# The sum over experts taken head by head: eight PSUM accumulations and eight VectorE additions per tile instead of one accumulation

## The reference, cut to what matters

```python
def block(args):
    xb, eb, gb = args            # 128 tokens, their experts (128, 8, 16), their gates
    ub = u_tab[eb]
    vb = v_tab[eb]
    act = jax.nn.gelu(jnp.einsum('td,thkd->thk', xb, ub), approximate=False)
    return jnp.einsum('thk,thkd->td', gb * act, vb)
...
h_lat = h_lat + g2 * y_lat
```

## Time and profile before

| | |
|---|---|
| runs of the kernel | 4520.79, 4525.88 and 4529.47 us, median 4525.88 |
| the profiled execution | 4520.79 us, its span in the profile 4519.0 us |
| TensorE, share of the span busy | 79% |
| VectorE | 61% |
| ScalarE | 26% |
| GpSimd | 34% |
| mean rate of the DMA | 322 GB/s over the span |
| mean granted TensorE clock | 0.931 of full speed |

### The profile page before, as it was taken

How to read it: one execution, slowest core, us unless ns; L and a number is a source line. 1 busy time by engine, 2 the same in 40 slices (tenths; PEclk the granted TensorE clock), 3 DMA queues, 4 the chain that set the end, 5 groups by cost and what they waited for, 6 DMA issues and landing times. The chain is left out here.

```text
span 4519.0 us, 38887 instructions
## 1 busy us (share of the span) xinstructions
PE 3574.6 (79%) x10024; PEld 1731.3 (38%) x10024; DVE 2775.2 (61%) x6957; ACT 1156.5 (26%) x2826; POOL 1527.8 (34%) x1338
## 2 busy tenths in 40 slices
PE   8899978778768768777777768996877876877776
PEld 1288643323323323323322227784332332332322
DVE  2222348776776676676676545664877677667654
ACT  1121013222222222222232122551322222222212
POOL 0102114444443444443344321000444444444432
PEclk9898589999999999998999998998999999999999
DMA  8712049999999999999999982003999999999998
GB/s 300 253 56 84 1 171 376 407 397 393 403 387 390 402 382 386 406 378 373 411 387 409 421 369 82 1 1 151 378 399 397 394 406 398 368 408 392 400 421 344
DMA packets 233035, 1455.51 MB, mean 322 GB/s; under 512 B 25140, under 2 KB 25140, under 8 KB 67812
## 3 DMA queue, kind: packets, MB, share of 16 engines
q0 software_dynamic: 184320, 1342.26, 73.2%
q1 hardware_dynamic: 48392, 110.79, 6.9%
q10 hardware_dynamic: 96, 0.10, 0.0%
HBM read 1447.72 MB, written 5.34 MB: 322 GB/s over the span
## 5 line engine op out<-in xcount | busy, mean ns | idle before, releaser
L1371 PE MATMUL peer_py<-peer_ring,peer_diag 128*128 128x512 f32 x5120 | 2470.4, 631 | 821.3 <-ACT peer_diag L1288 820.7
L1217 POOL DMA_INDIRECT peer_ring<-in_uv_dram,peer_idx x1280 | 1443.1, 1127 | 2008.6 <-PE peer_py L1371 1728.1
L1482 DVE CUSTOM_DVE_ANT_0 peer_ring<-peer_ring,peer_f 128x1024 f32<-128x1024 f32 x1280 | 1565.9, 1226 | 768.9 <-DMA peer_ring<-in_uv_dram,peer_idx 738.0
L1371 PEld LDWEIGHTS peer_py<-peer_ring,peer_diag 128*128 128x128 f32 x5120 | 983.0, 200 | 2277.4 <-ACT peer_diag L1288 1161.8
L1288 ACT ACTIVATE peer_diag<-ident,peer_coef 128x128 f32<-128x128 f32 x1280 | 443.9, 394 | 1813.0 <-DVE peer_coef L1458 1813.0
L1285 ACT ACTIVATE peer_gel<-peer_u 128x2 f32<-128x2 f32 x640 | 129.9, 203 | 711.4 <-DVE peer_u L1482 710.4
L318 DVE TENSOR_TENSOR m_w_low<-m_w_low_plain,m_w_high 128x2048 fp32r<-128x2048 f32 x26 | 61.0, 2347 | 218.5 <-ACT m_w_high L313 218.5
L1208 POOL IOTA peer_iota<- 128x16 f32 x2 | 0.3, 144 | 504.7 <-POOLq L765 363.9
L326 PE MATMUL m_ps<-m_w_high,m_aT_high 128*128 128x512 f32 x416 | 165.3, 397 | 3.3 <-DVE m_v L750 1.6
L326 PE MATMUL m_ps<-m_w_low,m_aT_high 128*128 128x512 f32 x416 | 163.1, 392 | 0.0
L326 PE MATMUL m_ps<-m_w_high,m_aT_low 128*128 128x512 f32 x368 | 144.5, 393 | 0.0
(11 more groups left out here) (196 smaller groups left out, 2824.9 us busy)
## 6 DMA issues: line engine op xcount, KB each, us to landing
arena<-in_ada_w_dram SPq DMA_DIRECT2D x16, 2048.0 KB, 8.8
peer_ring<-in_uv_dram,peer_idx POOLq DMA_INDIRECT x1280, 9.0
mod_rows_sb<-in_ada_w_dram SPq DMA_DIRECT2D x8, 2048.0 KB, 9.2
m_w_low_plain<-in_ev_w_in_dram SPq DMA_DIRECT2D x12, 1024.0 KB, 5.2
arena<-in_peer_wq_dram SPq DMA_DIRECT2D x2, 4096.0 KB, 19.2
mod_rows_sb<-mod_rows SPq DMA_DIRECT2D x7, 1024.0 KB, 7.1
m_w_low_plain<-in_od_w_in_dram SPq DMA_DIRECT2D x6, 1024.0 KB, 5.4
m_w_low_plain<-in_ev_w_out_dram SPq DMA_DIRECT2D x4, 1024.0 KB, 5.0
```

The lines of the kernel that those rows point to most:

```text
L1217: pool.indirect_dma_start(ring[:, s % RING], None, A["uv"], bass.IndirectOffsetOnAxis(idx[:, hd, j:j + 1], 0)).then_inc(sem(f"landed{s % R ...
L1371: ins = pe.matmul(PY[:, b], diag[:, s % RING], ring[:, s % RING, D + b * HALF:D + (b + 1) * HALF], start=s == 0, stop=s == TS - 1)
L1482: dve.tensor_tensor_reduce(x, x, f[:], 1.0, 0.0, ALU.mult, ALU.add, u[:, g % 4, j:j + 1]).then_inc(sem("dot"), 1)
```

## The change

`PY` becomes two pairs of banks. The slots of a head accumulate in one pair, the next head's in the other. When a head is complete, VectorE moves its sum out of PSUM: head 0 by a copy into `y`, heads 1 to 7 by an addition to `y` (`head_sum`). For heads 0 to 6 this stands behind the dots of pairs 11, 19, 27, 35, 43, 51 and 59, ahead of the routing piece of that pair; for head 7 at the end of the tile. TensorE waits for `y_free` at the start of each head, for the sum of the head two before it. The product with the gate row now reads `y` in SBUF and not PSUM, and raises a new semaphore, `gated`.

```diff
-        PY = ctx.enter_context(nc.psum_tensor(T + "py", [P, 2, HALF], F32))
+        PY = ctx.enter_context(nc.psum_tensor(T + "py", [P, 2, 2, HALF], F32))
...
             def body(i, now, nxt):
                 for g in range(PAIRS_T):
-                    if g == 0:
-                        pe.wait_ge(sem("y_free"), i + 1)
+                    hd = g // PAIRS
+                    if g % PAIRS == 0:
+                        pe.wait_ge(sem("y_free"), i * NH + hd + 1)
                     for j in range(PAIR):
                         s = PAIR * g + j
                         pe.wait_ge(sem("diag"), i * TS + s + 1)
                         for b in range(2):
-                            ins = pe.matmul(PY[:, b], diag[:, s % RING], ring[:, s % RING, D + b * HALF:D + (b + 1) * HALF],
-                                            start=s == 0, stop=s == TS - 1)
+                            ins = pe.matmul(PY[:, hd % 2, b], diag[:, s % RING], ring[:, s % RING, D + b * HALF:D + (b + 1) * HALF],
+                                            start=s % TOPK == 0, stop=s % TOPK == TOPK - 1)
...
+            def head_sum(i, hd):
+
+                dve.wait_ge(sem("slot_free"), i * TS + RING + (hd + 1) * TOPK)
+                ps = PY[:, hd % 2].rearrange("p b n -> p (b n)")
+                if hd == 0:
+                    dve.tensor_copy(y[:], ps).then_inc(sem("y_free"), 1)
+                else:
+                    dve.tensor_tensor(y[:], y[:], ps, ALU.add).then_inc(sem("y_free"), 1)
+
             if layer == 0:
-                dve.sem_inc(sem("y_free"), 1)
+                dve.sem_inc(sem("y_free"), 2)
...
+                    if g % PAIRS == 3 and g >= PAIRS:
+                        dve.wait_ge(sem("y_free"), i * NH + g // PAIRS + 1)
+                        head_sum(i, g // PAIRS - 1)
...
                 coefficients(i, PAIRS_T - 1)
-                dve.wait_ge(sem("slot_free"), i * TS + RING + TS)
+                dve.wait_ge(sem("y_free"), i * NH + NH + 1)
+                head_sum(i, NH - 1)
+                dve.wait_ge(sem("y_free"), i * NH + NH + 2)
+
                 if i is first:
                     dve.wait_ge(sem("gates"), 16 * rows_loads)
-                dve.tensor_tensor(y[:], PY[:].rearrange("p b n -> p (b n)"), rows[:, row_kind(i), 2], ALU.mult).then_inc(sem("y_free"), 1)
-                dve.wait_ge(sem("y_free"), i + 2)
+                dve.tensor_tensor(y[:], y[:], rows[:, row_kind(i), 2], ALU.mult).then_inc(sem("gated"), 1)
+                dve.wait_ge(sem("gated"), i + 1)
                 dve.tensor_tensor(h[:, i - shift], h[:, i - shift], y[:], ALU.add).then_inc(sem("h"), 1)
```

## The result

The changed kernel takes 4597.18 us (median of four runs, 4594.8 to 4603.24), the kernel before 4525.25 (four runs, 4520.79 to 4529.47). The ratio is 1.0166, 95% interval 1.0151 to 1.0180, or +72 us. The forecast was +46, with a range to 4597: the direction was right, and 26 us of the size are missing. The first question is where they lie.

What follows compares the result with a forecast made beforehand. The prediction took VectorE's program order as the bound in pairs 36 to 56, the gathers without routing, and a chain at tile ends. Terms 13.3 + 25.6 + 4.8 + 2.4 = 46.1 us on 4526 gave 4572, range 4552 to 4597.

Steps and rivals of the forecast that it cites:

- (a): Ten tile ends: head 7's sum lengthens the chain from last matmul to next dots; 13.3 us, between 12.2 and 13.7.
- (b): Pairs 35, 43, 51 in eight routing tiles: 24 sums of 1.2 us less 3.2 for the queue; 25.6 us, 18.4 to 32.9.
- The 2.18 us: Each sum's hold on VectorE by the skill's flush rule, in place of 1.2 us; the whole would then be 91 us.
- (c): Pairs 11 and 19 of tiles 0 and 6: four sums of 1.2 us with routing; 4.8 us, 2.3 to 5.5.
- (e): The other 34 sums, hidden in VectorE's waits for the DMA: nothing, at pair 59 up to 2 us in all.
- (d): Pair 11 in the other eight tiles: the gather delay just fits, 0.3 us each; 2.4 us, 0 to 9.6.
- The idle time at the loop's jump I leave as it is: At the loop's jump: the 5.58 us of idle before the copy of `f` stays unchanged, nothing added.
- nothing measurable: Rival: tile ends too are covered, by gathers still in flight; 4526 us, chance 0.04.
- faster: Rival: TensorE starts new tiles before `PY` is read, 1.22 us earlier at eight ends; 4516 us, chance 0.02.
- only the tile ends: Rival: delays inside a tile vanish in the gather queue, only ends cost 13 us; 4539 us, chance 0.08.
- every sum costs: Rival: gather-bound stretches have no real slack, so all 80 sums cost 1.2 us; 97 us, 4623, chance 0.03.
- holds VectorE for twice its length: Rival: each sum holds VectorE 2.45 us in place of 1.2; 103 us together, 4629, chance 0.02.

Runs made afterwards that it cites:

- e1: The kernel before with an added copy of PY to y at each tile's end, the product then reading y: 4544.27 us, ratio 1.0025 to the kernel before.
- e3: The changed kernel without the sums at pairs 35, 43 and 51: 4563.97 us, ratio 1.0072 to the kernel before.
- e7: The changed kernel with twelve semaphore increments, which do nothing and run once, ahead of the loop: 4591.64 us, ratio 1.0139 to the kernel before.
- e13: The kernel before with one unused 128x1024 VectorE addition from SBUF at pair 27 of each tile: 4527.53 us, ratio 1.0003.
- e4: The changed kernel without the sums at pairs 19, 27 and 59: 4587.84 us, ratio 1.0130 to the kernel before.
- e8: The kernel before with one unused 128x1024 VectorE addition from SBUF at pair 11 of each tile: 4541.25 us, ratio 1.0034.
- e5: The changed kernel with each sum inside a tile three pairs later (14, 22, ..., 62): 4581.59 us, ratio 1.0127 to the kernel before.
- e2: The changed kernel without the sums at pair 11: 4587.37 us, ratio 1.0119 to the kernel before.
- e11: The changed kernel with four unused TensorE matmuls at pair 10 in the eight tiles that route for a successor: 4599.36 us, ratio 1.0159 to the kernel before.
- e12: The changed kernel with the edits of e5 and e7 together: 4578.43 us, ratio 1.0109 to the kernel before.

## Why the prediction was right or wrong

**Right: (a).** Tile ends. 11 to 14 us alone (e1) against 13.3; per end 1.25 us written out, 1.46 in the loop (forecast 1.265 and 1.375).

**Right: (b).** Pairs 35, 43 and 51. 24.0 to 25.9 us in four traces, 30 by the times of e3 and e7 (33 with e3's rest of the stop), against 25.6. VectorE's order was the bound there. The deduction of 3.2 for the queue was a guess, and no run tests it alone; that the sum comes so close is in part luck. The 2.18 us would have made it 49: the flush rule of the Trainium skill, VectorE: DVE Perf Modes, section "The DRAIN you can't avoid", does not hold for a sum. The section itself excepts an operation that is not held, and the trace agrees with the exception: the instruction behind a sum starts 1.13 us after it.

**Right: (c) and (e).** 5.1 to 6.3 us against 4.8. The 34 sums taken as free are free as far as can be told: pairs 26 to 33 and the tiles 5 and 9 lie at or below zero, e13 gives 1 us (-3 to 6); e4's 4 to 6 us, of which 2.4 are pair 19 in tiles 0 and 6, have too wide an interval to say more. One trace has 8.7 us in pairs 57 to 63, another 2.5, a third 0.4; what happened in the first isn't known.

**Wrong in size: (d), "a delay of 1.2 just fits. I take 0.3 each".** It measured 17 to 20 us for eight tiles, where I had 2.4 and an upper end of 9.6. The slack that I worked out was not one. I took the 6.93 us from the issue of slot 30's gather to its dot, less 5.45 for a gather issued to idle queues, as time in which it could come later. In e8 the gather is issued 0.59 us before the dot of slot 28 instead of 1.95, 1.36 later, and the dot of slot 30 comes 1.44 later: from issue to dot it is 7.01 us, no less than before. All of a delay comes through. In the changed kernel's tile 2, where the issue is later still, the DMA engines go dry behind it (0.51 busy over 4 us); in e8's they are busy 0.96 and pass 348 GB/s in place of 418, and why the delay comes through there too is not shown. The upper end was too low as well, since a late gather comes with more than one delay.

I sorted tiles by when slot 30's gather was issued: the eight tiles of row (d), in eight traces without an instruction added at pair 11 and six with one. In the table are the pairs 14 to 26 in us, means over the tiles; gathers at full rate would need 12 x 4.97 = 59.6:

```
slot 30's gather issued, after
pair 12's first dot                4.65 to 4.72 us    5.07 to 6.51 us
nothing added at pair 11           60.37 (45 tiles)   61.81 (19 tiles)
one instruction added              61.54 (20 tiles)   63.54 (28 tiles)
```

Down a column it is 1.2 and 1.7 us, the delay itself. Along a row it is 1.4 and 2.0 us, and with the addition 28 of 48 tiles fall into the dearer class instead of 19 of 64. The delay, 1.2 to 1.7, and 0.29 x 1.8 = 0.5 make about 1.9 us a tile, 15 us for eight. By the times it is 13 to 18 us: e8's 15 less 2.4 for tiles 0 and 6, e5's 18, and e2's 18 with its stop taken off, less the same 2.4. That the delay is what costs is shown, by e8 (put in) and by e5 and e2 (taken away).

That the dearer class comes of the clock is shown by the same 14 traces, by the clock over the matmuls themselves. In all 112 tiles pair 11's matmuls begin 1.85 to 1.92 us after the first dot of pair 12, and the gather is issued 0.97 to 1.02 us after the four of slot 22, which free its buffer. In the 65 tiles of the first column these four take 1.82 us at a granted clock of 1.00, in the 47 of the second 2.20 to 3.58 us at 0.50 to 0.83; no tile falls between. (The lower level alone does not tell: 47 of the 65 had it too for a while, but earlier, as in tile 2 of the kernel before at pair 10.) And e11's six tiles with the clock at 1.00 show, in one trace, that an issue made late by other means is as dear. Two things stay open. Why the lower level meets pair 11 more often with the addition, 28 times in 48 against 19 in 64, is not shown: the idle time ahead of pair 11's matmuls was 1.93 to 4.64 us in the late tiles and 0.76 to 3.77 in the others. And only two tiles, in e11, had the clock kept up there without a delay from the filler.

**Left out: "The idle time at the loop's jump I leave as it is".** This is the second step that failed. The 5.6 us there are indeed unchanged (22.4 us at four jumps, 22.5 before), but behind them came another stop of 4.0 to 4.6 us at three jumps, 13 us in all, a wait that the sum put at nothing. e7 shows what decides it: not what the sums do but where in the code the loop begins. In e2, with one sum less ahead of the loop, it stands one instruction later and is 3 us long; in e3 and e4, with three less, 0.8 to 1.0 us are left of it behind the third dot. That the engine waits there for its instructions to be fetched is the reading that fits, but no run shows it; which boundary the loop's start crossed isn't known, and so I could not have said whether this change would meet it.

**The whole.** By the times: ends 12, the stop 12, pairs with routing 33 (25 by the traces), pair 11 in all tiles 15, pair 19 in tiles 0 and 6 another 2, together 74, or 66 by the traces' 25. Measured were 72 and 77, each with an interval of some 7 us on either side. The kernel is slower for the reason that was given, and the increase is over half as much again for two terms that stood at 2.4 and at nothing. Of the rivals, "nothing measurable" and "faster" fall by the result, "only the tile ends" by rows (b) and (d), "every sum costs" by e13 and "holds VectorE for twice its length" by the starts 1.13 us apart.

None of the versions beats the kernel before. The best of those that have all sums is e12, 1.1% slower: three sums a tile stand where VectorE is the bound, and one at the end of the chain.

## What to carry to other kernels

Time from issue to use, less the shortest such time seen, is not slack: here a gather issued 1.36 us later was used 1.44 us later. Where an instruction is added ahead of a transfer that an engine is soon going to wait for, price the delay in full, and look whether it comes with a second one, as here by TensorE's clock (1.82 or up to 3.58 us for the same four matmuls). In a chain that runs from a dot through a matmul to the next gather, the place of an instruction decides: the same 1.2 us cost 1.6 us at pair 11 and next to nothing at pairs 14 or 27. When code is added to a kernel with hardware loops, look at the first instructions behind each jump before explaining the rest, several of them, since a stop can move behind the next one, and compare ablations only between kernels with the same stops there.

## What was not expected of the hardware

A jump of a hardware loop costs VectorE 5.4 to 6.2 us of idle time in each of the kernels here, and a further 3.6 to 4.6 us ahead of the next instruction in some: 4.59, 4.33 and 4.00 in one trace, 4.59, 4.31 and 4.35 in another, 2.9 to 3.2 us one instruction later still in e2, and none at all with twelve small instructions more ahead of the loop (1.0168 against 1.0139).

Addition and product of 128x1024 float32 take the same with an operand in PSUM (1.216 and 1.225 us) as from SBUF alone (1.220 in e8, 1.225 in the changed kernel). A copy does not: 1.221 us out of PSUM, 0.69 us from SBUF to SBUF, as that of `f`.

TensorE's matmuls behind a wait of 4.64 us began at 0.50 of the full clock where those behind one of 0.94 us ran at 1.00: sixteen matmuls took 9.75 us there and 7.13 here.

```profile
1444.43 9.75 PE L1372 MATMUL peer_py<-peer_ring,peer_diag 128*128 128x512 f32 x16 [4.64 <-ACT peer_diag L1288]
```

```profile
1415.34 7.13 PE L1371 MATMUL peer_py<-peer_ring,peer_diag 128*128 128x512 f32 x16 [0.94 <-ACT peer_diag L1288]
```

The first of these is the changed kernel's at pairs 11 and 12 of tile 2, the second the kernel before at the same place.
